# Two-layer blocks on one core: at layer borders the two token tiles are skewed, and the norm is applied by VectorE ahead of plain transposes

## The reference

```python
def rmsnorm(x, g):
    xf = x.astype(jnp.float32)
    y = xf * lax.rsqrt(jnp.mean(xf * xf, axis=-1, keepdims=True) + NORM_EPS)
    return (y * g.astype(jnp.float32)).astype(x.dtype)
...
        h = rmsnorm(x, norm_g[i, 0]) * (1.0 + scale_t) + shift_t
...
        x = x + gate_t * y
        h = rmsnorm(x, norm_g[i, 1]) * (1.0 + scale_c) + shift_c
        y = jnp.square(jax.nn.relu(h @ mlp_w1[i])) @ mlp_w2[i]
        x = x + gate_c * y
    return rmsnorm(x, final_g)
...
    for i in range(DEPTH):
        x = x + mixer(_rmsnorm(x, norm[i]))
        x = x + _conv_ffn(_rmsnorm(x, ffn_norm[i]), ...)
    return _rmsnorm(x, final_norm)
```

## Time and profile before

| what | value |
|---|---|
| median of 3 runs | 1440.84 us (1439.13 to 1441.12) |
| the profiled execution | 1442.56 us, span 1440.7 us |
| TensorE matmul busy | 1374.8 us (95%) |
| TensorE weight load busy | 1207.1 us (84%) |
| VectorE busy | 937.0 us (65%) |
| ScalarE busy | 664.8 us (46%) |
| GpSimd busy | 81.6 us (6%) |
| TensorE in the chain that ended last | 89% of the span |
| waits of TensorE for the diagonals (line 1627, by DVE nd) | 16.1 us, 13 times |

### The profile page before, as it was taken

One profiled execution on the slowest core, in us unless ns is written; L12 is line 12 of the kernel. 1 busy time (PEld: TensorE's weight loads), 2 busy tenths in 40 slices (PEclk: granted clock), 3 DMA queues, 4 the chain that ended last, 5 costly groups with the idle time before them and its releaser, 6 DMA issues.

```text
span 1440.7 us, 20830 instructions
## 1 busy us (share of the span) xinstructions
PE 1374.8 (95%) x8456; PEld 1207.1 (84%) x8456; DVE 937.0 (65%) x1128; ACT 664.8 (46%) x809; POOL 81.6 (6%) x150
## 2 busy tenths in 40 slices
PE   5999899999999899999799999999999999999996
PEld 1797799998787679999698878899998987899996
DVE  4697676875797776555675345677677434677674
ACT  1543444444546454444434354554455457554452
POOL 1111100100111110000100010000000000000000
PEclk9899999999999899999999999999999999999998
DMA  9786267864695246555365434454553541454530
GB/s 369 265 345 254 100 238 286 310 233 176 244 357 202 91 181 243 198 178 177 116 209 199 161 132 175 147 204 176 180 196 123 207 144 49 157 204 176 179 143 30
DMA packets 46092, 279.23 MB, mean 194 GB/s; under 512 B 5200, under 2 KB 5200, under 8 KB 18880
## 3 DMA queue, kind: packets, MB, share of 16 engines
q1 hardware_dynamic: 33264, 231.57, 44.4%
q0 software_dynamic: 12752, 46.57, 8.7%
HBM read 277.07 MB, written 1.05 MB: 193 GB/s over the span
## 4 chain that ended last, share of the span: by engine, by line
PE 89%; DVE 5%; ACT 2%; issue 1%; DMA 1%; POOL 1%; SPq 0%; POOLq 0%; DVEq 0%; ACTq 0%
PE ps L1566 42%; PE ps L1603 13%; PE ps L1605 13%; PE ps L1604 13%; PE ps L1665 1%; DMA ada<-in_ada_w 1%; DVE h_lo L986 1%; PE ps L1627 1%; POOL rstd L499 1%; PE ps L2005 1%; PE ps L1638 1%; DVE x L1027 1%; DVE h_hi L985 1%; ACT h L600 1%; DVE xn L1023 0%
## 5 line engine op out<-in xcount | busy, mean ns | idle before, releaser
L932 DVE TENSOR_TENSOR w_lo<-raw,w_hi 128x2048 fp32r<-128x2048 f32 x210 | 479.9, 2290 | 213.1 <-ACT w_hi L575 212.2
L575 ACT ACTIVATE w_hi<-raw 128x2048 fp32r<-128x2048 f32 x210 | 400.8, 1911 | 336.6 <-PE ps L1566 289.7
L1603 PE MATMUL ps<-h_hi,w_hi 128*128 128x256 f32 x1536 | 437.2, 285 | 6.3 <-DVE h_lo L986 5.6
L1605 PE MATMUL ps<-h_hi,w_lo 128*128 128x256 f32 x1536 | 435.3, 283 | 0.0
L1604 PE MATMUL ps<-h_lo,w_hi 128*128 128x256 f32 x1536 | 435.3, 283 | 0.0
L1603 PEld LDWEIGHTS ps<-h_hi,w_hi 128*128 128x128 f32 x1536 | 293.5, 191 | 11.7 <-issue 6.6
L1604 PEld LDWEIGHTS ps<-h_lo,w_hi 128*128 128x128 f32 x1536 | 293.5, 191 | 2.0
L1605 PEld LDWEIGHTS ps<-h_hi,w_lo 128*128 128x128 f32 x1536 | 293.5, 191 | 0.0
L1566 PE MATMUL ps<-w_hi,h_hi 128*128 128x512 f32 x448 | 151.8, 400 | 1.0 <-DVE h_lo L986 1.0
L1566 PE MATMUL ps<-w_hi,h_lo 128*128 128x512 f32 x448 | 148.4, 392 | 0.0
L1566 PE MATMUL ps<-w_lo,h_hi 128*128 128x512 f32 x448 | 148.2, 392 | 0.0
(11 more groups left out here) (249 smaller groups left out, 1114.8 us busy)
## 6 DMA issues: line engine op xcount, KB each, us to landing
raw<-in_stream SPq DMA_DIRECT2D x210, 1024.0 KB, 4.9
ada<-in_ada_w POOLq DMA_DIRECT2D x80, 512.0 KB, 6.3
ada<-in_ada_w SPq DMA_DIRECT2D x8, 512.0 KB, 13.5
raw<-in_ada_w SPq DMA_DIRECT2D x8, 512.0 KB, 15.8
row<-in_gate_b POOLq DMA_DIRECT2D x3, 512.0 KB, 3.5
x<-in_x SPq DMA_DIRECT2D x1, 1024.0 KB, 10.7
retc<-in_retc POOLq DMA_DIRECT2D x1, 1024.0 KB, 5.3
out<-xn SPq DMA_DIRECT2D x2, 512.0 KB, 2.7
```

The lines of the kernel that those rows point to most:

```text
L575: act.activation(w_hi[:, s, :], raw[:, s, :], ACT.Copy).then_inc(hi_done[s], 1)
L932: dve.tensor_tensor(w_lo[:, s, :], raw[:, s, :], w_hi[:, s, :].bitcast(f32), ALU.subtract)\
L1603: pe.matmul(out, wh, h_hi[:, kt, :], start=kt == 0, stop=False)
L1605: last = pe.matmul(out, wl, h_hi[:, kt, :], start=False, stop=kt == KT - 1)
```

## The change

At the seven borders the two tiles go one behind the other, so that one tile's norm runs while TensorE multiplies for the other.

- The last two row chunks of a layer are interleaved (`last_two`): all of both chunks for bank 0, then for bank 1, for bank 2, and for bank 3. In the middle of bank 3, tile 0's transposes are put.
- VectorE scales the tile (`scale_tile`, x times rstd into `xn`), and TensorE transposes it with the identity (`norm_tile`). ScalarE's evacuation and VectorE's split are done per tile, on 128 columns each.
- The first two column chunks of the next layer are multiplied tile by tile (`first_two`), with tokens as the stationary operand and 256 weight columns streaming, into banks 0 to 3, token by feature. ScalarE evacuates the four quarters to `fc` (`evacuate`, with the relu where an MLP follows), and TensorE transposes them back (`turn`). Where the layer starts with row chunks (border 2), `first_rows` does the first two by tile.
- Border 4 multiplies by the final gain before the inverse norms are known (`add_final`), squares both versions, takes both means at once (`both_means`), and scales twice (`both_scales`).
- The weight copies `hi` and `lo` of the next layer's third and fourth chunk stand behind this in the engines' orders. The first MLP's and second MLP's `lo(c0 + 4)` and `hi(c0 + 4)` stand behind the second unit. The gate row of borders 1 and 3 is multiplied before the last two chunks, that of border 4 one unit earlier.
- At the end, the last two chunks are interleaved too, and tile 0 is normalized before the adds of tile 1.

```diff
+            def last_two(a, b, lhs, ready, between):
+                slots = chunk_ready(a), chunk_ready(b)
+                for t in range(TT):
+                    for n in range(2):
+                        for second, s in enumerate(slots):
+                            if t == n == 0 and second:
+                                pe.wait_ge(*ready)
+                            for k in range(2):
+                                high, low = lhs(second, k, t)
+                                for p in range(3):
+                                    w = (w_hi, w_lo, w_hi)[p][:, s, k * D + n * 512:k * D + (n + 1) * 512]
+                                    last = pe.matmul(ps[:, 2 * t + n, :], (high, high, low)[p], w, start=False,
+                                                     stop=second == k == 1 and p == 2)
+                            if t == n == 1 and not second:
+                                last.then_inc(used[s], 1)
+                                between()
+                        if 2 * t + n < 3:
+                            last.then_inc(y_part, 1)
+                last.then_inc(used[slots[1]], 1)
+
+            def norm_tile(k, t):
+                pe.wait_ge(nd_done, TT * k + t + 1)
+                for kt in range(KT):
+                    last = pe.transpose(ps[:, 4 + 2 * t + kt // 4, (kt % 4) * P:(kt % 4 + 1) * P],
+                                        xn[:, t, kt * P:(kt + 1) * P], ident)
+                    if kt % 4 == 3:
+                        last.then_inc(tr_done, 1)
+
+            def first_two(c0, k, stage, i):
+                slots = chunk_ready(c0), chunk_ready(c0 + 1)
+                for t in range(TT):
+                    for second, s in enumerate(slots):
+                        for kt in range(KT):
+                            if not second and kt % 2 == 0:
+                                pe.wait_ge(hl_done, split_of(stage, t, kt // 2))
...
+                            for p in range(3):
+                                w = (w_hi, w_lo, w_hi)[p][:, s, kt * T:(kt + 1) * T]
+                                last = pe.matmul(ps[:, 2 * t + second, 0:T], (high, high, low)[p], w,
+                                                 start=kt == p == 0, stop=kt == KT - 1 and p == 2)
+                            if second and t == 0 and kt == 2:
+                                norm_tile(k, 1)
+                            if second and t == 1 and kt == 1:
+                                turn(i, 0)
+                        last.then_inc(used[s] if t else fc_mm, 1)
+
+            def turn(i, which):
+                pe.wait_ge(fc_done, 4 * i + 3 + which)
+                for f in range(2):
+                    for t in range(TT):
+                        last = pe.transpose(ps[:, 4 + which, f * T + t * P:f * T + (t + 1) * P],
+                                            fc[:, which, t, f * P:(f + 1) * P], ident)
+                last.then_inc(fc_tr, 1)
...
-                up(B, 0, c0, False, stage)
-                up(B + 1, 1, c0 + 1, False)
+                first_two(c0, 1 + 2 * layer, stage, layer)
                 down(B, 0, c0 + 2, True, False)
+                turn(layer, 1)
...
-                down(B + UNITS - 1, (UNITS - 1) % 2, c, False, True)
+                pe.wait_ge(hid_done, B + UNITS - 1)
+                last_two(c - 1, c, hidden, (hid_done, B + UNITS), lambda: norm_tile(2 + 2 * layer, 0))
...
+                last_two(ffn_chunk(c0, GROUPS - 2, 2), ffn_chunk(c0, GROUPS - 1, 2), hidden, (hid_done, done),
+                         (lambda: norm_tile(6, 0)) if layer == 0 else (lambda: None))
```

ScalarE's order at a border (`square`, `norm_tile` and `evacuate` are its own helpers; `k == 4` is border 4):

```diff
+            def boundary(k, x_count, stage, scale_col, bias_col, c0, first=None, func=ACT.Copy):
+                square(x_count, 0)
+                if k == 4:
+                    square_scaled(0)
+                square(x_count, 1)
...
+                square(x_count, 2)
...
+                norm_tile(stage, 0, scale_col, bias_col)
+                square(x_count, 3)
...
+                hi(c0 + 2)
+                if first is not None:
+                    evacuate(first, 0, (fc_mm, 2 * first + 1), func)
+                norm_tile(stage, 1, scale_col, bias_col)
+                if first is not None:
+                    evacuate(first, 1, (fc_mm, 2 * first + 2), func)
+                hi(c0 + 3)
+                if first is not None:
+                    evacuate(first, 2, multiplied(c0), func)
+                    evacuate(first, 3, multiplied(c0 + 1), func)
...
-                unit(B, 0, False, c0)
+                unit(B, 0, False, (fc_tr, 2 * layer + 1))
+                unit(B + 1, 1, False, (fc_tr, 2 * layer + 2))
                 hi(c0 + 4)
-                unit(B + 1, 1, False, c0 + 1)
```

VectorE's order, the scaling, and the first units of an MLP:

```diff
+            def scale_tile(k, t):
+                dve.wait_ge(rstd_done, TT * k + t + 1)
+                dve.tensor_scalar(xn[:, t, :], x[:, t, :], rstd[:, t:t + 1], None, ALU.mult).then_inc(nd_done, 1)
...
+            def boundary(add, y, k, stage, c0):
+                add(y, 0)
+                add(y, 1)
+                norm_mean(k, 0)
+                scale_tile(k, 0)
+                add(y, 2)
+                split_tile(stage, 0, 0, 3)
+                add(y, 3)
+                split_tile(stage, 0, 3, 1)
+                norm_mean(k, 1)
+                scale_tile(k, 1)
+                split_tile(stage, 1, 0, 4)
+                lo(c0 + 2)
+                lo(c0 + 3)
...
                 unit(B, 0)
-                lo(c0 + 4)
                 if layer == 1:
                     steps(11 * KT, 2)
                 unit(B + 1, 1)
+                lo(c0 + 4)
                 lo(c0 + 5)
                 if layer == 1:
                     steps(11 * KT + 2, 3)
```

More of the change, by code:

```diff
@@ L378, in build @@
         BY_DVE = [Y_GR, Y_GOUT, Y_M0, Y_DOUT, Y_M1, Y_ROUT, Y_F0, Y_SOUT, Y_F1]
-        X_GLA, X_M0, X_DIFF, X_M1, X_FG, X_RET, X_F0, X_SB, X_F1 = 4, 8, 12, 16, 18, 22, 26, 30, 34
+        X_GLA, X_M0, X_DIFF, X_M1, X_RET, X_F0, X_SB, X_F1 = range(4, 36, 4)
+        NORM_STAGES = (TR_N1, TR_N2, TR_N3, TR_N4, TR_N5, TR_N6, TR_N7)
+        HL_BASE = [sum(8 if s in NORM_STAGES else 4 for s in range(stage)) for stage in range(13)]
         N_C_RET = 4
@@ L575, in hi @@
                 act.activation(w_hi[:, s, :], raw[:, s, :], ACT.Copy).then_inc(hi_done[s], 1)
-            def squares(k, x_count, dst=sq_out):
-                for n in range(4):
-                    t, half = n // 2, n % 2
-                    if x_count == X_FG:
-                        act.wait_ge(x_done, X_FG - 1 + t)
-                    elif x_count is not None:
-                        act.wait_ge(x_done, x_count - 3 + n)
-                    part = slice(half * 512, (half + 1) * 512)
-                    act.activation(dst[:, t, part], x[:, t, part], ACT.Square, scale=D ** -0.5,
-                                   accum_out=ssq[:, 2 * half + t:2 * half + t + 1]).then_inc(ssq_done, 1)
@@ L589, in norm, with square @@
-            def norm(k, x_count, stage, late, scale_col, bias_col):
-                squares(k, x_count)
-                hi(late)
-                norm_rows(stage, scale_col, bias_col)
+            def square(x_count, n, dst=sq_out):
+                t, half = n // 2, n % 2
+                if x_count:
+                    act.wait_ge(x_done, x_count - 3 + n)
+                part = slice(half * 512, (half + 1) * 512)
+                act.activation(dst[:, t, part], x[:, t, part], ACT.Square, scale=D ** -0.5,
+                               accum_out=ssq[:, 2 * half + t:2 * half + t + 1]).then_inc(ssq_done, 1)
@@ new lines, in square_scaled, with norm_tile @@
+            def square_scaled(n):
+                t, half = n // 2, n % 2
+                act.wait_ge(xf_done, n + 1)
+                part = slice(half * 512, (half + 1) * 512)
+                act.activation(sq_fg[t][:, half, :], xn[:, t, part], ACT.Square, scale=D ** -0.5,
+                               accum_out=ssq[:, 6 + 2 * half + t:7 + 2 * half + t]).then_inc(ssq_done, 1)
+            def norm_tile(stage, t, scale_col, bias_col):
+                for b in range(4):
+                    if b % 2 == 0:
+                        act.wait_ge(tr_done, 4 * stage + 2 * t + b // 2 + 1)
+                    for kt in (2 * b, 2 * b + 1):
+                        src = ps[:, 4 + 2 * t + kt // 4, (kt % 4) * P:(kt % 4 + 1) * P]
+                        last = act.activation(h32[:, kt, t * P:(t + 1) * P], src, ACT.Identity,
+                                              bias=bias_col(kt) if bias_col else 0.0, scale=scale_col(kt))
+                    last.then_inc(hh_done, 1)
@@ L634, in _ @@
             act.wait_ge(x_in, 16)
-            squares(0, None, xn)
+            for n in range(4):
+                square(None, n, xn)
             act.wait_ge(small_in, 16 * 7)
@@ L909, in _ @@
             hi(C_SV + 7)
-            for c in range(C_SO, C_SO + 3):
-                hi(c + 4)
```

(10 more changed lines are left out.)

317 lines of the change are left out of this document (185 added, 132 removed).

## The result

The changed kernel took 1444.08 us (median of 12 runs, 1441.19 to 1447.05), the kernel before beside it 1440.65 us (12 runs, 1439.02 to 1442.33): ratio 1.0019, 95% interval 1.0012 to 1.0026. It is 3.4 us slower where 6.2 us faster was forecast, and lies outside the range of 1429 to 1441. Its profiled execution took 1445.26 us, span 1443.5.

A forecast was written before the change was run, and what follows sets the result against it. TensorE, chunk behind chunk, was taken as the bound, so gains lie at the borders. Border terms 0.2 + 2.3 - 2.15 + 2.2 + 3.3 - 0.3 + 3.3 - 2.6 = 6.25 us, off 1440.84, gave 1434.6; range 1429 to 1441.

The forecast's parts named there:

- each new wait: TensorE idles: 2.65 us before both MLPs' first down-chunk, 2.35 before the second's third, 3.6 at both FFN ends.
- a rival at 0.2: Clock falls to half at the two 3.6 us FFN-end stalls, costing up to 4 us: 1438.3; chance 0.2.
- What bounds the kernel: TensorE, chunk behind chunk, away from the borders; the seven borders hold 57.6 us extra that a perfect skew could take.
- the plain borders: Borders 5 and 7, without a gate: extra falls from 6.6 to 3.2 us, 3.3 saved at each.
- Borders 2, 5 and 7: Savings of 2.3 us at border 2, which starts with row chunks, and 3.3 us at each of the others.
- border 4: The border with the final gain: extra falls from 13.9 to 11.7 us, 2.2 saved.
- half tiles don't get shorter: At all borders, evacuation and split keep their cost per instruction and scaling takes 1.28 us: 18 us slower, 1453; chance 0.06.
- Border 1: GLA to MLP, with gate: extra falls from 8.2 to 8.0 us, including 2.65 before the first down-chunk; 0.2 saved.
- Border 3: Gate, second MLP follows: like border 1, plus 2.35 us idle at the third down-chunk behind VectorE's ada steps; loses 2.15.
- Border 6 and the end: A 3.6 us wait for each FFN's last hidden group: 0.3 lost at the border, 2.6 at the kernel's end.
- a half granted clock at border 6: Listed sign of a wrong forecast: TensorE's clock at half at border 6, where a 3.6 us idle was expected.
- plain transposes: At the borders, one instruction instead of two: both tiles' transposes take 1.7 us instead of 4.1 for diagonal products.

The follow-up runs named there:

- run four: Changed kernel plus unused matmuls: 18 before each MLP's first down-chunk, 24 before each FFN's last hidden group; 1436.02 us, ratio 0.9959.
- run three: Changed kernel with VectorE's eight ada steps in the second MLP dealt as 4, 2, 2 instead of 2, 3, 3; 1440.38 us, ratio 0.9989.
- run five: Changed kernel with the sum of the tenth ada part moved behind the second chunk of the value rows; 1443.29 us, ratio 1.0016.
- run eight: Kernel before with only the scaling on VectorE and plain transposes instead of diagonal products, no skew; 1451.84 us, ratio 1.007.
- run nine: Run eight's kernel with the transposes written as products with the identity; 1446.01 us, ratio 1.0036.
- run one: Changed kernel with ScalarE's first unit of both MLPs ahead of its evacuation of the fourth quarter; 1439.47 us, ratio 0.9983.
- run six: Changed kernel with the changes of run one, run two, run three and run five together; 1426.77 us, ratio 0.9904.
- run seven: Run six's kernel with the sum of the tenth ada part left where the changed kernel has it; 1427.52 us, ratio 0.9903.
- run ten: Run six's kernel plus 18 unused matmuls ahead of the first tile's transposes at border 4; 1426.02 us, ratio 0.9895.
- run two: Changed kernel with each FFN's last two down-chunks one after the other again, first tile's transposes in the last bank; 1437.2 us, ratio 0.9969.

## Why the prediction was wrong, point by point

**The step that failed.** The sum charged each new wait (2.65 us at the MLPs, 2.35 at the third unit, 3.6 at the ends of the FFNs) with its own length and nothing for TensorE's clock behind it; the clock stood only in a rival at 0.2. The traces show 10.5 us lost to half clock behind these waits, and run four gives back 8.6 us by filling four of the five without shortening one. Two smaller terms were left out: the late ada rows (1.0 us) and the sum in the differential attention (3.2 us in one trace).

**What bounds the kernel; the plain borders.** Right. Borders 2, 5 and 7 gave 2.2, 3.7 and 3.7 us for 2.3, 3.3 and 3.3, border 4 2.8 for 2.2. The sizes of the new pieces held. After, VectorE and TensorE at border 5:

```profile
911.48 0.75 DVE L1046 TENSOR_SCALAR xn<-x,rstd 128x1024 f32<-128x1024 f32 x1 [0.67 <-POOL rstd L516]
914.36 0.29 DVE L1063 CAST h_hi<-h 128x256 fp32r<-128x256 f32 x1 [1.53 <-ACT h L620]
915.03 0.29 DVE L1063 CAST h_hi<-h 128x256 fp32r<-128x256 f32 x1
913.06 1.04 PE L1701 MATMUL ps<-shp,xn 128*128 128x128 f32 x8
```

The scaling took 0.75 us (taken: 0.7), a split pair comes every 0.67 us (914.36 to 915.03; taken: 0.67), eight transposes 1.04 with the overhang, and they start without a wait. The rival "half tiles don't get shorter" is out by these rows.

**Border 1: the step that failed is the end of its sum.** The wait before the first down-chunk was forecast at 2.65 us and is about 2.4. What was left out is what the idle does to the work behind it: 24 matmuls in 7.34 instead of 5.49 us, 1.85 us. This is the price when the fall comes: in the traces of runs three and five the same idle of 2.42 us stood here and the clock stayed full. I had put the clock into a rival with two places, and these weren't the two.

**Border 3: the same twice, and a stall too small.** 7.37 and 7.36 us for 5.49 make 3.75 us; the stall of 2.35 was 3.34, since the ada rows came 1.14 us late, a load that I had not followed. 2.15 + 3.75 + 1.0 make 6.9; measured are 6.2.

**Border 6 and the end: the rival happened.** The idle was sized well, 3.45 for 3.6 us. Behind it 36 matmuls took 11.23 us instead of 36 x 0.229 = 8.2, and 18 took 6.01 instead of 4.1: 3.0 and 1.9 us. With the forecast's +0.3 and +2.6 and the 0.15 us that the idle was shorter this makes 3.15 and 4.35; measured are 2.7 and 4.4. The last power took 0.55 us, as said. The prediction had named a half granted clock at border 6 as a sign that it is wrong.

**Diff attention, charged at nothing.** No step of mine followed what border 2's gain would bring in front of. The steps of VectorE for the tenth ada part ended at 427.1 instead of 428.9, but TensorE came to the sum 3.5 us earlier, stood 1.90 us and then worked at half clock until 435.3: 3.2 us in that trace. Moving the sum back removed this in the trace, and little in the medians, so this term is the least certain. The fall isn't new either: in the kernel before, TensorE idles 0.31 us ahead of the same sum, and its clock falls behind it as well, for 3.2 us. The lines (timeline of TensorE, and a stretch as in the earlier trace rows) were in the trace of before when the prediction was made:

```profile
429.10 1.92 PE L1638 MATMUL ps<-shp,acc 128*128 128x1 f32 x16 [0.31 <-issue]
432.00:435.20 3.20, 3.20 (x9) 2.44 (x8) 3.20 (x5) 0.00 (x0) 0.16 (x1) 0.50 0.90 319
```

So of the 3.2 us, 1.6 are the longer idle and the rest is a half-clock stretch that is 6.6 us long instead of 3.2.

**The clock's share.** 1.85 + 3.75 + 3.0 + 1.9 = 10.5 us lost to half clock at the five places of the MLPs and FFNs. Run four, which fills all of them but the third unit of the second MLP, and so leaves 1.87 of it, gives back 8.6 measured for 10.5 - 1.9 = 8.6 us. That they agree to the digit is luck, since the measured one is known to about 2 us. The forecast of -6.25 with these 10.5 is +4.2. The rest of the table nearly cancels: +3.2 (diff attention) and +1.0 (the late load) against -2.4 ahead of border 1 and some 3.2 in small amounts at the borders, together -1.4, which gives the +2.8 of the spans. The -2.4 and the 3.2 in small amounts are remainders of one pair of executions, not terms that a run shows. So the chance of 0.2 for "the clock falls" was wrong above all. The argument against it was that idles of 1 to 1.3 us had left the clock full, and that the only fall looked at stood behind a longer one. Between 1.3 and 3.6 us no row was read, and I treated the MLPs' 2.65 us as harmless without one. There were such rows: besides the sum above, the trace of before has an idle of 2.00 us at 457.57 in the differential attention, and the clock at 0.54 from 459.3 to 463.0 behind it. The Trainium skill ("TensorE: Matmul & The Clock Gate", Why this matters for your kernels) warns of idle gaps between bursts; the traces agree, at 2.42 us in 6 of 8 cases. A slip besides: the rival's own terms, 1434.6 and 4 us, make 1438.6 and not 1438.3.

**The skew itself gains**, as the sum had it: the scaling alone costs 10 us, the skew on top of it wins back 7 of them, and with the order mended it wins 24. Of the 10 us, 5.3 came with the plain transposes (runs eight and nine), which the sum had booked as a gain; what the skew does with the old products was not run.

## What to carry to other kernels

Price a new idle of TensorE as the idle plus what the clock may take behind it (here 1.9 to 3.0 us for idles of 2.4 to 3.5 us in front of dense work, in most executions but not in all), look for the clock in the whole trace of before and not at one place, and use several executions, since one trace has falls that the next has not; a few unused matmuls in the gap tell the two shares apart. When a stage is made earlier, follow every wait that its engine meets next: the result it needs is made by an engine that did not get faster. Where work moves out of a matmul onto another engine, ask what TensorE still does in that time, since the cheaper instruction can be the slower kernel.

## What the runs showed of the hardware

- In after the granted clock fell to half behind idles of 1.90, 2.42, 3.34 and 3.45 us, for 3.4 or 6.6 us each, and did not behind idles of 1.15 to 1.2 us (runs one and after).
- The same idle brings a fall in one execution and none in another. Counted over the traces of the twelve kernels, as far as each has the idle:

| idle of TensorE | where | half clock behind it |
|---|---|---|
| 1.15 us | first down-chunk of both MLPs (runs one, six, seven, ten) | 0 of 8 |
| 2.00 us | differential attention, 457.57 in before (all twelve) | 11 of 12 |
| 2.42 us | first down-chunk of both MLPs (after, runs two, three, five) | 6 of 8 |
| 2.5 us | border 4 (after, runs one to seven) | 2 of 8 |
| 3.45 us | last hidden group of both FFNs (after, runs one, three, five) | 8 of 8 |

- A long idle isn't needed: soon after the sum of an ada part (16 matmuls of one column, 1.9 us) the clock fell with only 0.31 us of idle ahead of the sum (before, 432.0) and with 0.19 us (run six, near 405). The cause wasn't tried.
- It also fell at borders with no idle over 1.9 us, where TensorE ran only light transposes between short waits (run eight), and stayed up when these were written as products of twice the length (run nine): 1451.84 against 1446.01 us.
- A GpSimd power that took 1.54 us at the end of the kernel before, beside a scalar-tensor-tensor of 1024 elements on VectorE (1431.12 for 1.28 us), took 0.55 in after, where none runs beside it; the cause wasn't tried by itself.
- A tensor-scalar of 1024 fp32 elements a partition with a scalar per partition took 0.75 us, a scalar-tensor-tensor of the same size 1.285.
